# Last layer of a three-layer block: queries transposed one projection tile later, gates and last keys finished elsewhere, compressed scores by head pairs, their transposes in a free bank

## The reference

```
y = rmsnorm(x, norm_mix) @ od_w_in            # 1024 -> 2608 columns
qc, kc_raw, vc_raw, ks, vs, kw, vw, gc = split_cols(y, ODD_SPLITS)   # 1024, 6 x 256, 48
q = rope(qc)                                  # 16 heads of 64, in 4 groups
k_cmp = compress(rope(kc_raw), pe[0], w1[0], w2[0])   # 15 keys a group
v_cmp = compress(vc_raw, pe[1], w1[1], w2[1])
k_slc, k_win = rope(ks), rope(kw)             # 256 keys a group, each
gates = sigmoid(gc)                           # 3 per head
o = g0 * softmax(q k_cmp) v_cmp + g1 * softmax(q k_slc) vs + g2 * softmax(q k_win) vw
x = x + o @ od_w_out
x = x + swiglu(rmsnorm(x, norm_ffn), ...)     # then rmsnorm(x, norm_final)
```

## Time and profile before

| | us |
|---|---|
| runs | 1165.88, 1171.35, 1180.18 |
| profiled execution, its own time | 1171.34 |
| its span | 1169.6 |
| PE busy | 1007.5 (86%) |
| PE weight loads busy | 723.1 (62%) |
| DVE busy | 592.3 (51%) |
| ACT busy | 484.7 (41%) |
| POOL busy | 98.5 (8%) |

### The profile page before, as it was taken

One profiled execution on the slowest core, in us unless ns is written; L12 is line 12 of the kernel. 1 busy time (PEld: TensorE's weight loads), 2 busy tenths in 40 slices (PEclk: granted clock), 3 DMA queues, 4 the chain that ended last, 5 costly groups with the idle time before them and its releaser, 6 DMA issues. The chain is left out here.

```text
span 1169.6 us, 20145 instructions
## 1 busy us (share of the span) xinstructions
PE 1007.5 (86%) x8483; PEld 723.1 (62%) x8483; DVE 592.3 (51%) x955; ACT 484.7 (41%) x791; POOL 98.5 (8%) x110
## 2 busy tenths in 40 slices
PE   6987899978676667998789999997986878999996
PEld 5565788555333333886537777766874545877774
DVE  5574478541000003688565555436646876555453
ACT  6454354310000004455466445515433656555532
POOL 3500090000000001034000000002040000000000
PEclk9896699989778899998898999998987998999998
DMA  8812003999999995552092765515411046655530
GB/s 270 267 56 79 1 4 108 423 405 421 421 421 421 421 413 187 158 177 76 1 341 98 245 199 190 190 66 176 138 59 73 1 139 240 213 196 188 193 108 36
DMA packets 108325, 228.56 MB, mean 195 GB/s; under 512 B 7145, under 2 KB 86044, under 8 KB 93660
## 3 DMA queue, kind: packets, MB, share of 16 engines
q1 hardware_dynamic: 105275, 219.38, 51.6%
q0 software_dynamic: 2976, 8.14, 2.3%
HBM read 224.63 MB, written 1.05 MB: 193 GB/s over the span
## 5 line engine op out<-in xcount | busy, mean ns | idle before, releaser
L518 DVE SCALAR_TENSOR_TENSOR ffn_wu_lo<-ffn_w_up,ffn_wu_hi 128x2048 f16<-128x2048 f32 x44 | 99.0, 2288 | 55.5 <-ACT ffn_wu_hi L443 55.5
L1118 PE MATMUL rw_pB<-ring,kept 128*32 128x256 f32 x864 | 79.3, 479 | 43.2 <-DMA ring<-in_w_up 21.2
L656 PE MATMUL ffn_pG<-ffn_hT_hi,ffn_wu_hi 128*128 128x256 f16 x352 | 97.9, 278 | 3.8 <-DVE ffn_hT_lo L560 3.8
L656 PE MATMUL ffn_pG<-ffn_hT_lo,ffn_wu_hi 128*128 128x256 f16 x352 | 97.9, 278 | 0.0
L656 PE MATMUL ffn_pG<-ffn_hT_hi,ffn_wu_lo 128*128 128x256 f16 x352 | 97.8, 278 | 0.0
L656 PE MATMUL ffn_pU<-ffn_hT_lo,ffn_wu_hi 128*128 128x256 f16 x352 | 96.0, 273 | 0.0
L656 PE MATMUL ffn_pU<-ffn_hT_hi,ffn_wu_hi 128*128 128x256 f16 x352 | 96.0, 273 | 0.0
L656 PE MATMUL ffn_pU<-ffn_hT_hi,ffn_wu_lo 128*128 128x256 f16 x352 | 96.0, 273 | 0.0
L1118 PEld LDWEIGHTS rw_pB<-ring,kept 128*32 128x32 f32 x864 | 42.2, 137 | 76.3 <-issue 67.2
L443 ACT ACTIVATE ffn_wu_hi<-ffn_w_up 128x2048 f16<-128x2048 f32 x44 | 81.7, 1900 | 2.5 <-DMA ffn_w_up<-in_ffn_w_gate 2.3
L243 DVE SCALAR_TENSOR_TENSOR in_w_lo<-wt,in_w_hi 128x2048 f16<-128x2048 f32 (+2 forms) x22 | 52.9, 2403 | 42.8 <-ACT in_w_hi L236 42.3
(11 more groups left out here) (639 smaller groups left out, 2175.9 us busy)
## 6 DMA issues: line engine op xcount, KB each, us to landing
ring<-in_w_gate SPq DMA_DIRECT2D x27, 1024.0 KB, 26.2
ring<-in_w_up SPq DMA_DIRECT2D x27, 1024.0 KB, 26.4
ring<-in_w_down SPq DMA_DIRECT2D x26, 1024.0 KB, 26.6
ffn_w_up<-in_ffn_w_gate SPq DMA_DIRECT2D x22, 1024.0 KB, 7.6
ffn_w_up<-in_ffn_w_up SPq DMA_DIRECT2D x22, 1024.0 KB, 9.9
ffn_w_down<-in_ffn_w_down SPq DMA_DIRECT2D x22, 1024.0 KB, 5.1
wt<-in_ev_w_in SPq DMA_DIRECT2D x9, 1024.0 KB, 5.5
wt<-in_od_w_in SPq DMA_DIRECT2D x9, 1024.0 KB, 5.3
```

Of the source, the lines that this page charges most:

```text
L518: return nc.vector.scalar_tensor_tensor(out, whole, scale, hi, ALU.mult, ALU.subtract)
L656: ins = T.matmul(p[:, s, j * SEQ:(j + 1) * SEQ], w[:, s, m, c, j::NJ], h[:, c, :], start=(n == 0), stop=(n == 3 * KC - 1))
L1118: ins = nc.tensor.matmul(into[i * CAP:(i + 1) * CAP, 0:D_EXPERT], h[:, c, i * CAP:(i + 1) * CAP], held[:, c * D_EXPERT:(c + 1) * D_EXPERT] ...
```

## The change

In the input stage the query transposes go behind tile 7 (PE), and their copy to `qT` behind ACT's high part of tile 9, ahead of the doubling of the selected keys. `kcT` becomes a block pattern, each group's keys once in rows 0 to 63 and once in rows 64 to 127 with zeros beside, written by two half-height copies; POOL clears it at the stage's start. The last two key copies go one to DVE, one to ACT. The gates' exponential and + 1 leave this stage.

In the attention stage the gates are finished first, with a new semaphore `gate_exps`. A compressed score covers both heads of a pair: 16 calls of 128 rows and 32 columns in place of 32 of 64 rows and 16 columns, into one bank. PE waits for `c_masked` behind the score of unit 2. DVE copies `left(1)` ahead of the compressed weights. The transposes of the compressed weights go to bank 1 of `pO`, without the two waits for the copies of unit 2, and DVE copies them out ahead of `weigh(3)` and `left(2)`.

```diff
@@ odd_in, scalar: waits and copies of q
-                        if k == 7:
+                        if k == 8:
                             act.wait_ge(q_turned, 1)
...
-                    act.wait_ge(pr.moved, n_tiles)
-                    nc.scalar.activation(o.gates[:], y[:, :, 2560:2608], ACT.Exp, scale=-1.0).then_inc(gate_exps, 1)
+                    act.wait_ge(kw_turned, 1)
+                    copy(keys_of(1, 1), sc[:, 3, :]).then_inc(kw_out, 1)
@@ odd_in, vector
-                            nc.vector.tensor_copy(o.kcT[:], sc[:, 2, 0:C_G * CMP_KEYS])
+                            dve.wait_ge(glink, 1)
+                            for i in range(2):
+                                own = slice(i * C_DIM, (i + 1) * C_DIM)
+                                nc.vector.tensor_copy(o.kcT[own, :, i, :], sc[own, 2, 0:C_G * CMP_KEYS].rearrange("p (g k) -> p g k", g=C_G))
...
-                    keys_out(1, kw_turned, kw_out)
-                    dve.wait_ge(gate_exps, 1)
-                    nc.vector.tensor_scalar(o.gates[:], o.gates[:], 1.0, None, ALU.add).then_inc(vlink, 1)
+                    dve.wait_ge(kw_turned, 1)
+                    nc.vector.tensor_copy(keys_of(1, 0), sc[:, 2, :]).then_inc(kw_out, 1)
@@ odd_in, tensor: the 16 transposes of q
-                        if k == 6:
+                        if k == 7:
                             pe.wait_ge(q_roped, 1)
                             pe.wait_ge(c_out, 1)
@@ sparse_attention, scalar and vector, at their start
+                    nc.scalar.activation(gates[:], y[:, :, 2560:2608], ACT.Exp, scale=-1.0).then_inc(gate_exps, 1)
...
+                    dve.wait_ge(gate_exps, 1)
+                    link(nc.vector.tensor_scalar(gates[:], gates[:], 1.0, None, ALU.add))
@@ sparse_attention, vector, loop over u
+                        if u == 2:
+                            dve.wait_ge(c_turned, 1)
+                            nc.vector.tensor_copy(cT[:].rearrange("p i s -> p (i s)"), pO[:, 1, :]).then_inc(c_out, 1)
                         if u + 1 < units:
                             weigh(u + 1)
+                        left(u)
                         if u == 1:
                             compressed_weights()
-                        left(u)
-                        if u == 2:
-                            dve.wait_ge(c_turned, 1)
-                            nc.vector.tensor_copy(cT[:], pT[:, :, 0:SEQ]).then_inc(c_out, 1)
@@ sparse_attention, tensor
-                            for i in range(2):
-                                own = slice(i * C_DIM, (i + 1) * C_DIM)
-                                at = (t * PAIRS + n) * CMP_KEYS
-                                g = n // per_group
-                                ins = nc.tensor.matmul(pT[:, i, at:at + CMP_KEYS], qT[own, n, t * P:(t + 1) * P],
-                                                       kcT[own, g * CMP_KEYS:(g + 1) * CMP_KEYS], start=True, stop=True,
-                                                       skip_group_check=True)
+                            at = (t * PAIRS + n) * 2 * CMP_KEYS
+                            ins = nc.tensor.matmul(pT[:, 0, at:at + 2 * CMP_KEYS], qT[:, n, t * P:(t + 1) * P],
+                                                   kcT[:, n // per_group].rearrange("p i k -> p (i k)"), start=True, stop=True,
+                                                   skip_group_check=True)
                     ins.then_inc(c_scored, 1)
-                    pe.wait_ge(c_masked, 1)
                     for u in range(units):
                         if u + 2 < units:
                             score(u + 2)
+                        if u == 0:
+                            pe.wait_ge(c_masked, 1)
                         turn(u)
                         if u == 2:
-                            pe.wait_ge(probs_left, 3)
-                            pe.wait_ge(probs_right, 3)
                             pe.wait_ge(c_weighed, 1)
                             for i in range(2):
                                 for t in range(TT):
-                                    ins = nc.tensor.transpose(pT[:, i, t * P:(t + 1) * P],
-                                                              cS[:, i, t].rearrange("p n k -> p (n k)"), ident)
+                                    at = i * SEQ + t * P
+                                    ins = nc.tensor.transpose(pO[:, 1, at:at + P], cS[:, i, t].rearrange("p n k -> p (n k)"), ident)
                             ins.then_inc(c_turned, 1)
                             pe.wait_ge(c_out, 1)
```

More of the change, by code:

```diff
@@ L3193, in __init__ @@
         self.qT, self.kT = sb("qT", [P, PAIRS, SEQ]), sb("kT", [P, 2, C_G, SEQ])
-        self.kcT, self.vc = sb("kcT", [P, C_G * CMP_KEYS]), sb("vc", [P, PAIRS, C_DIM])
+        self.kcT, self.vc = sb("kcT", [P, C_G, 2, CMP_KEYS]), sb("vc", [P, PAIRS, C_DIM])
         self.gates = sb("gates", [P, TT, 3 * C_H])
@@ L3212, in odd_in @@
         sc = pr.pT
+        keys_of = lambda b, n: o.kT[:, b, 2 * n:2 * n + 2, :].rearrange("p g s -> p (g s)")
         side = ["rows_in", "emb_turned", "emb_out", "kc_roped", "c_twice", "x_turned", "x_lower", "x_upper", "hidden",
                 "gelus", "seconds", "c_out", "q_roped", "q_turned", "q_out", "ks_roped", "kw_roped", "ks_twice", "kw_twice",
-                "ks_turned", "kw_turned", "ks_out", "kw_out", "gate_exps", "vlink", "glink", "alink"]
+                "ks_turned", "kw_turned", "ks_out", "kw_out", "vlink", "glink", "alink"]
         with Stage(nc, "in3", Projection.NAMES + side) as sems:
@@ L3219, in odd_in @@
              q_roped, q_turned, q_out, ks_roped, kw_roped, ks_twice, kw_twice, ks_turned, kw_turned, ks_out, kw_out,
-             gate_exps, vlink, glink, alink) = sems[len(Projection.NAMES):]
+             vlink, glink, alink) = sems[len(Projection.NAMES):]
             with nc.Block(no_gpsimd_drain=True) as block:
@@ L3231, in _ @@
                     nc.gpsimd.memset(hidV[:], 0.0)
+                    nc.gpsimd.memset(o.kcT[:], 0.0)
                     link(nc.gpsimd.memset(xp[:], 0.0))
@@ L3301, in _ @@
                     link = Link(dve, vlink)
[L3303 to L3308, removed]
                     pr.begin_dve(dve)
@@ L3335, in _ @@
                         if k == 9:
-                            keys_out(0, ks_turned, ks_out)
-                    keys_out(1, kw_turned, kw_out)
-                    dve.wait_ge(gate_exps, 1)
-                    nc.vector.tensor_scalar(o.gates[:], o.gates[:], 1.0, None, ALU.add).then_inc(vlink, 1)
+                            dve.wait_ge(ks_turned, 1)
+                            nc.vector.tensor_copy(keys_of(0, 0), sc[:, 0, :])
+                            nc.vector.tensor_copy(keys_of(0, 1), sc[:, 1, :]).then_inc(ks_out, 1)
+                    dve.wait_ge(kw_turned, 1)
+                    nc.vector.tensor_copy(keys_of(1, 0), sc[:, 2, :]).then_inc(kw_out, 1)
                 @block.tensor
@@ L3426, in sparse_attention @@
                                "probs_left", "probs_right", "summed", "high_out", "low_out", "c_scored", "c_masked",
-                               "c_less", "c_exped", "c_weighed", "c_turned", "c_out", "vlink"]) as sems:
+                               "c_less", "c_exped", "c_weighed", "c_turned", "c_out", "gate_exps", "vlink"]) as sems:
             (scored, least, exped, weighed, probs_turned, probs_left, probs_right, summed,
-             high_out, low_out, c_scored, c_masked, c_less, c_exped, c_weighed, c_turned, c_out, vlink) = sems
+             high_out, low_out, c_scored, c_masked, c_less, c_exped, c_weighed, c_turned, c_out, gate_exps, vlink) = sems
             with nc.Block(no_gpsimd_drain=True) as block:
@@ L3519, in compressed_scores @@
                             ins = nc.vector.tensor_tensor(
-                                cS[:, i], pT[:, i, 0:TT * P].rearrange("p (t n k) -> p t n k", t=TT, k=CMP_KEYS), mask,
+                                cS[:, i], pT[:, 0, :].rearrange("p (t n i k) -> p i t n k", t=TT, i=2, k=CMP_KEYS)[:, i], mask,
                                 ALU.add)
```

## The result

The changed kernel took 1158.12 us (median of 4 runs, 1152.65 to 1165.56) against 1173.53 of the kernel before (4 runs): ratio 0.987, 95% interval 0.982 to 0.992. The forecast was 1158.3, the range 1151 to 1167. A second set gave 1160.37 (6 runs), ratio 0.990 (0.985 to 0.995). The medians of the first set lie 15.4 us apart. Over all sets the means are 1172.68 (34 executions of before, one that ran over 1.5% above the fastest left out) and 1159.67 (10 of after), 13.0 us apart; the sum had said 13.05.

A forecast was written before the change was run, and what follows sets the result against it. The end follows one chain through the last stage, nearly all PE's SwiGLU matmuls, so ending the two changed stages earlier moves it equally. Gains 6.4 + 0.95 + 0 + 5.7 = 13.05 us gave 1158.3 us, range 1151 to 1167.

The forecast's parts named there:

- Part 1: Input stage, query transposes behind tile 7: gain 6.4 us from 3.76 idle, 2.49 slow clock and 0.17 overlap.
- cover: Input stage: ACT's and POOL's work moved behind tile 7 is ready before PE wants it, the tightest by 0.9 us.
- Part 2: End of the input stage: last key copies shared by DVE and ACT, gates gone; gain 0.95 us, at least 0.3.
- Part 3: Attention stage's start: 1.8 us of gates work ahead of the first smallest, hidden behind the first score; cost 0.
- the cap that was named: Attention stage's start: at full clock the 1.8 us gates chain would limit the gain from that clock.
- K: Stretch from the attention stage's first matmul to the start of smallest(5): 28.07 us before, 22.4 predicted.
- Part 4: Compressed scores: full-height block at 4.1 us gains nothing; the order behind it brings smallest(2) 0.7 us earlier.
- The mask wait: Attention stage: PE no longer waits 1.05 us for the mask before score(2); smallest(2) starts 0.7 us earlier.
- Part 5: Attention units 1 and 2: earlier compressed transposes and copy; smallest(5) 5.7 us earlier together with Part 4's 0.7.
- The sign named for it: Attention stage from first to last matmul: 5.7 us shorter than the 70.9 before.
- The clock: Attention stage rivals: slow first units 1160 to 1163, chance 0.22; everything full clock 1156, 0.13; lower clock throughout 1182, 0.02.
- L: Stretch from the start of smallest(5) to the end of the last attention matmul: predicted unchanged at 42.8 us.

The follow-up runs named there:

- e1: Kernel before with only the query transposes put behind tile 7, their copies one step later; 1169.56 us, ratio 0.996 (0.992 to 1.000).
- e2: Changed kernel with both last key copies back on DVE and the gates finished in the input stage again; one execution, K 20.10 us.
- second profile: The changed kernel profiled once more, without any edit; K 21.73 us.
- e8: Changed kernel with one small early exponential on ACT, loading the table in the input stage; one execution, K 24.63 us.
- e3: Kernel before with the attention stage's edits alone, queries, gates and last keys as before; 1169.38 us, ratio 0.998 (0.994 to 1.002).
- e4: Changed kernel with compressed scores again as 32 calls of 64 rows and 16 columns; one execution, block 3.78 us, K 21.48 us.
- e5: Changed kernel with PE waiting for the mask again ahead of score(2); one execution, K 24.90 us.
- e7: Changed kernel with the compressed transposes back in the unit turns' banks, both waits and the late copy restored; one execution, K 27.16 us.
- e6: Changed kernel with left(1) again behind the compressed weights; one execution, K 26.35 us.
- e10: Changed kernel with e8's early table load and score(5) ahead of the wait for the compressed probabilities' copy; 1160.08 us, ratio 0.989 (0.984 to 0.994).
- e11: Changed kernel with 8 unused bfloat16 matmuls of 512 columns among the 16 compressed score calls; one execution, block 4.82 us, K 23.20 us.
- e12: e10 with the compressed block split, 8 calls ahead of score(2) and 8 behind unit 0's turn; 1159.06 us, ratio 0.987 (0.982 to 0.992).

## Why the prediction was right

- **Part 1**, 6.4: measured 6.44 in e1 and after. The idle time and the slow clock behind it were both real, and no cover broke.
- **Part 2**, 0.95: 0.96 (e2).
- **Part 3**, 0: right where the clock is 0.50 in the first score (first `smallest` 1.86 behind the first matmul in the second profile, 2.22 before); at 1.00 it is the cap that was named (1.81 against e2's 1.28), and it vanished in DVE's later waiting, since e2 has the same K.
- **Part 4**: a full-height record at 1.00 costs 3.60 / 32 = 113 ns; 114 was taken. The 63 ns read for the half-height form mix two clocks, as the 4.06 us of the earlier trace rows ran at 1.00 and then at 0.50. The reason given, that half-height loads go side by side, is borne out by the loads of e1 and e8. The gain of 0.7 was 0.5 in e3, since the mask started 8.23 behind the first matmul, not at 7.9. The mask wait was worth 0.9 at `smallest(2)` and 1.6 at `smallest(4)` with the clock at 0.50 behind the block; 0.7 was taken.
- **Part 5**: 4.2 from `smallest(4)` to `smallest(5)` in six profiles (both of after, e2, e3, e4, e8). The working gave 902.3 - 898.1 = 4.2. The sign named for it, the attention stage 5.7 shorter than 70.9, came out as 6.3 in both profiles of after and as 3.8 in e3.
- **The clock** was mis-sized as a risk, not as a term. I had it as rivals beside the forecast, one case or another; the traces show that it varies from execution to execution of one kernel. In 29 executions of before the time goes with the mean granted clock (correlation -0.89, 6 us for 0.01; 1163.5 us at 0.934, 1180.9 at 0.909), and so does it in those of after.
- **Luck.** The agreement of one median with one number to 0.2 us is luck: single executions of the changed kernel lie between 1152.7 and 1165.6, and in the profiled one K was 2.3 better than forecast while L and the rest of the program gave 1.6 and 1.5 back. Parts 1, 2 and 5 are shown by the traces each for itself; that their sum is the whole gain is shown by the whole only.

What stays open: what sets the clock's fall, since e2 kept 1.00 across 2.75 us and others lost it within 1.7 us behind a pause of 1.79; whether the longer L belongs to the change; and why e1 and e3 together gained only half of what was expected in the runs.

## What to carry to other kernels

A hole of TensorE can be worth its length plus what the following work loses at half clock, and both can be read from the rows before the edit. Where a step reuses a bank that the pipeline needs, a free bank can be worth more than a faster instruction: here, with the order it allows, it carried nearly all of the gain from `smallest(4)` to `smallest(5)`, and the new matmul form none. When the clock differs between executions, compare stretches between fixed events of the program, and only those with the same granted clock; the totals can't separate edits of a few us.

## What was not expected of the hardware

A run of small float32 matmuls without a gap did not hold the clock: in all eight profiles in which the whole block met 1.00, the clock fell within it or within 1 us behind it (before, both of after, e2, e3, e4, e5, e7), and in the four others it ran at 0.50 for all its 6.85 us although PE was busy throughout (e1, e6, e8, e10). Only with the fillers (e11) or with the block in two halves (e12) did the clock outlast it, once each. That alone makes K of nearly the same code differ by 4.5 us (after and e8: 15.90 and 20.43 to `smallest(4)`).
